# A two-layer decoder trunk on one Trainium2 core: the last two expert pairs of each layer, and the turn into the next norm

## The reference

```python
for l in range(2):
    h = h + token_mixer(rms_norm(h, ln1_g[l]), w_in[l], ...)   # u @ w_in, 4 mixers, gated merge
    h = h + hier_moe(rms_norm(h, ln2_g[l]), ..., w1[l], w3[l], w2[l])
return rms_norm(h, final_g)

# hier_moe: every token goes to the 2 best of 32 experts (within its best group of 8)
hdn = jax.nn.silu(xb @ w1[e]) * (xb @ w3[e])      # 1024 -> 256
ys  = hdn @ w2[e]                                 # 256 -> 1024
out = zeros((T + 1, D)).at[slot_tok].add(ys * slot_w[:, None])[:T]
```

## Time and profile before

| | us |
|---|---|
| median of 3 runs | 1532.07 |
| lowest, highest | 1530.59, 1535.13 |
| the profiled execution | 1531.59 |
| its span, first to last instruction | 1529.8 |

### The profile page before, as it was taken

One profiled execution on the slowest core, in us unless ns is written; L12 is line 12 of the kernel. 1 busy time (PEld: TensorE's weight loads), 2 busy tenths in 40 slices (PEclk: granted clock), 3 DMA queues, 4 the chain that ended last, 5 costly groups with the idle time before them and its releaser, 6 DMA issues.

```text
span 1529.8 us, 18813 instructions
## 1 busy us (share of the span) xinstructions
PE 1377.0 (90%) x7414; PEld 952.2 (62%) x7414; DVE 429.2 (28%) x1017; ACT 506.0 (33%) x845; POOL 495.8 (32%) x249
## 2 busy tenths in 40 slices
PE   5999999999999799787589999999999978988783
PEld 5889877788887333232278888777888863333231
DVE  3232644411214111101433335443112241111105
ACT  4522466622333111111144326665223322111111
POOL 3633433466641111110054443334656311111100
PEclk9999999999998899999899999999999979999997
DMA  7622222224363999999844222222434649999985
GB/s 241 237 84 83 70 69 76 82 84 159 122 232 140 394 417 417 415 417 413 293 172 158 84 66 93 70 69 70 149 112 154 236 198 403 416 417 417 415 340 192
DMA packets 135089, 331.80 MB, mean 217 GB/s; under 512 B 16291, under 2 KB 90067, under 8 KB 116568
## 3 DMA queue, kind: packets, MB, share of 16 engines
q1 hardware_dynamic: 124920, 310.08, 53.8%
q0 software_dynamic: 10080, 20.49, 3.5%
HBM read 312.16 MB, written 34.60 MB: 227 GB/s over the span
## 4 chain that ended last, share of the span: by engine, by line
PE 70%; SPq 16%; DMA 7%; DVE 3%; ACT 2%; issue 1%; POOL 0%; DVEq 0%; POOLq 0%; ACTq 0%
PE ps L515 17%; PE ps L516 17%; PE ps L517 17%; SPq L437 11%; PE ps L852 9%; DMA w<-in_w 5%; SPq L431 5%; PE ps L681 2%; PE ps L661 1%; PE ps L669 1%; PE ps L617 1%; DMA xg<-x_dram,toks 1%; PE ps L770 1%; DVE ut L1351 1%; PE ps L844 1%
## 5 line engine op out<-in xcount | busy, mean ns | idle before, releaser
L515 PE MATMUL ps<-uH,ringH 128*128 128x512 f32 x720 | 281.9, 392 | 0.0
L516 PE MATMUL ps<-uL,ringH 128*128 128x512 f32 x720 | 280.4, 389 | 0.0
L517 PE MATMUL ps<-uH,ringL 128*128 128x512 f32 x720 | 280.3, 389 | 0.0
L852 PE MATMUL ps<-w,xT 128*64 128x512 f32 x1024 | 243.3, 630 | 39.7 <-DMA w<-in_w 37.2
L852 PEld LDWEIGHTS ps<-w,xT 128*64 128x64 f32 x1024 | 82.0, 145 | 197.3 <-issue 193.9
L852 PE MATMUL ps<-w,hT 128*64 128x512 f32 x512 | 121.0, 616 | 52.0 <-ACT hT L1167 29.1
L1231 POOL TENSOR_TENSOR ringL<-raw,ringH 128x2048 fp32r<-128x2048 f32 (+1 forms) x31 | 138.1, 4465 | 86.5 <-ACT ringH L975 86.5
L515 PEld LDWEIGHTS ps<-uH,ringH 128*128 128x128 f32 x720 | 135.2, 188 | 29.0 <-issue 0.7
L517 PEld LDWEIGHTS ps<-uH,ringL 128*128 128x128 f32 x720 | 135.1, 188 | 28.5
L516 PEld LDWEIGHTS ps<-uL,ringH 128*128 128x128 f32 x720 | 135.2, 188 | 27.7
L1277 POOL TENSOR_TENSOR ringL<-raw,ringH 128x2048 fp32r<-128x2048 f32 x32 | 146.9, 4590 | 5.1 <-ACT ringH L1101 5.1
(11 more groups left out here) (250 smaller groups left out, 2031.9 us busy)
## 6 DMA issues: line engine op xcount, KB each, us to landing
w<-in_w SPq DMA_DIRECT2D x188, 1024.0 KB, 21.5
raw<-in_w_in SPq DMA_DIRECT2D x54, 1024.0 KB, 5.3
y_dram<-attT SPq DMA_DIRECT2D x8, 1024.0 KB, 12.1
braw<-in_w_branch SPq DMA_DIRECT2D x32, 256.0 KB, 4.4
raw<-in_w_out SPq DMA_DIRECT2D x8, 1024.0 KB, 5.2
yb<-y_dram SPq DMA_DIRECT2D x8, 1024.0 KB, 7.9
h_dram<-hs SPq DMA_DIRECT2D x2, 2048.0 KB, 11.2
hs<-h_dram SPq DMA_DIRECT2D x2, 2048.0 KB, 9.9
```

The costliest lines, as they stand in the source:

```text
L515: mm(o, h, rh, start=first, stop=False)
L516: mm(o, h, rl_, start=False, stop=False)
L517: return mm(o, l, rh, start=False, stop=last)
L852: ins = mm(o[r], lhs[:, r], rhs[x], start=first, stop=last, skip_group_check=True)
```

## The change

`NS` becomes 14, so only the pairs 0 to 13 are scattered and the read-back waits for pair 13's scatter. Pair 14's rows go the way of pair 15's: `yH`, `yL` and `tok_of` exist twice. PE multiplies the first half of the columns of pair 14 into the banks in front of its wait for the last w2 (`combine_early`), the second half together with pair 15's. SP issues `yb` as soon as pair 13's rows are stored (the last two blocks also wait for pair 14's up product), then `raw`, `g1`, and the last w2. DVE adds the first two-part row in pair 14's turn, ahead of pair 15's gate product, and makes both low halves of pair 15 ahead of the adds. In the second layer the split of unit 1 (ACT and POOL) stands ahead of the norm. The means stand ahead of the products in `first_rows`' loop. The turn of row block 3 stands ahead of the second product block of `half(0)`, in both layers.

```diff
 CAP, NW = 64, 8
-SLOTS, NS = 3, NP - 1
+SLOTS, NS = 3, NP - 2
 EPS = 1e-6
...
     yy = [sb(f"yy{x}", [P, D], f32, R_O + 4 * x * KB) for x in range(2)]
-    yH = sb("yH", [P, D], f32r, R_O + 4 * (NS % 2) * KB)
+    yH = [sb(f"yH{x}", [P, D], f32r, R_O + 4 * x * KB) for x in range(2)]
     xT = [sb(f"xT{x}", [P, D], f32, R_O + (8 + 4 * x) * KB) for x in range(2)]
...
     tok_w = sb("tok_w", [P, S], f32r, R_O + 29.25 * KB)
-    yL = sb("yL", [P, D], f32r, R_T1)
-    tok_of = sb("tok_of", [P, S], f32r, R_T1 + 8 * KB)
+    yL = [sb(f"yL{x}", [P, D], f32r, R_T1 + 4 * x * KB) for x in range(2)]
+    tok_of = [sb(f"tok_of{x}", [P, S], f32r, R_T1 + (8 + 2 * x) * KB) for x in range(2)]
     yHw = sb("yHw", [P, D], f32r, R_T1 + 12 * KB)
...
                 w13_fill(p)
-                if p < NS:
+                if p < NP - 1:
                     hold(sp, down_filled.h, down_filled.at(lay, p - SLOTS + 1))
...
-            if lay + 1 < L:
-                hold(sp, up_filled.h, up_filled.at(lay, NP - 2))
-                sp.dma_start(raw[:, 0, :].rearrange("p (k n) -> p k n", k=KD), w_in_cols(lay + 1, COL["gv"], 256)).then_inc(w_in_slot[0].h, 16)
-            hold(sp, down_filled.h, down_filled.at(lay, NP - 2))
-            sp.dma_start(g1[:], a["c_next_gain"][ds(lay, 1), :].partition_broadcast(P)).then_inc(g1_in.h, 16)
+            hold(sp, down_filled.h, down_filled.at(lay, NS))
             for x in range(2):
...
             for t in range(NT):
+                if t == 2:
+                    hold(sp, up_filled.h, up_filled.at(lay, NS + 1))
                 sp.dma_start(yb[t][:], y_dram[2 * P * t:2 * P * (t + 1), :].rearrange("(p c) n -> p c n", c=2)).then_inc(y_back[t].h, 16)
-            hold(sp, down_filled.h, down_filled.at(lay, NP - SLOTS))
+            if lay + 1 < L:
+                sp.dma_start(raw[:, 0, :].rearrange("p (k n) -> p k n", k=KD), w_in_cols(lay + 1, COL["gv"], 256)).then_inc(w_in_slot[0].h, 16)
+            sp.dma_start(g1[:], a["c_next_gain"][ds(lay, 1), :].partition_broadcast(P)).then_inc(g1_in.h, 16)
             for c in range(2):
                 for x in range(2):
-                    src = a["w2"][ds(lay, 1), ds(NS + NP * x, 1), :, c * 512:(c + 1) * 512].rearrange("o q (k p) n -> p (o q k) n", p=P)
-                    sp.dma_start(w2[NS % SLOTS][x][:, :, c * 512:(c + 1) * 512], src).then_inc(w2_last_in[c].h, 16)
+                    src = a["w2"][ds(lay, 1), ds(NP - 1 + NP * x, 1), :, c * 512:(c + 1) * 512].rearrange("o q (k p) n -> p (o q k) n", p=P)
+                    sp.dma_start(w2[(NP - 1) % SLOTS][x][:, :, c * 512:(c + 1) * 512], src).then_inc(w2_last_in[c].h, 16)
...
                         if q < 2:
-                            if 1 <= 2 * q + i < NT - 1:
-                                norm_transposes(2 * q + i + 1, rows_low)
+                            if q == 0 and i == 1:
+                                norm_transposes(2, rows_low)
                             hold(pe, rows_low.h, rows_low.at(lay, 2 * q + i + 1))
+                            if q == 0 and i == 1:
+                                norm_transposes(3, rows_low)
                         for k in range(KD):
...
+            def token_rows(y, c, t, first, last):
+                mm(bank(SUM_BANKS[c][t]), tok_of[y][:, tmc(t)], yH[y][:, c * 512:(c + 1) * 512], start=first, stop=False, skip_group_check=True)
+                return mm(bank(SUM_BANKS[c][t]), tok_of[y][:, tmc(t)], yL[y][:, c * 512:(c + 1) * 512], start=False, stop=last, skip_group_check=True)
+
+            def combine_early():
+
+                hold(pe, last_low.h, last_low.at(lay, 1))
+                hold(pe, tokens_ready.h, tokens_ready.at(lay, 1))
+                for t in range(NT):
+                    token_rows(0, 0, t, True, False)
+
             def combine_last(c):
-                hold(pe, last_low.h, last_low.at(lay, c + 1))
-                hold(pe, tokens_ready.h, tokens_ready.at(lay, 1))
+                hold(pe, last_low.h, last_low.at(lay, c + 2))
+                hold(pe, tokens_ready.h, tokens_ready.at(lay, 2))
                 for t in range(NT):
...
                         hold(pe, half_added.h, half_added.at(lay, NT))
-                    b = SUM_BANKS[c][t]
-                    mm(bank(b), tok_of[:, tmc(t)], yH[:, c * 512:(c + 1) * 512], start=True, stop=False)
-                    mm(bank(b), tok_of[:, tmc(t)], yL[:, c * 512:(c + 1) * 512], start=False, stop=True).then_inc(sum_filled.h, 1)
+                    if c:
+                        token_rows(0, c, t, True, False)
+                    token_rows(1, c, t, False, True).then_inc(sum_filled.h, 1)
...
                 pe.wait_ge(hidden_copied.h, hidden_copied.at(lay, p + 1))
-                if p < NS:
+                if p < NP - 1:
                     pe.wait_ge(w2_in[s].h, w2_in[s].at(lay, 32 * (p // SLOTS + 1)))
...
                 else:
+                    combine_early()
                     for c in range(2):
...
+            if lay:
+                split_h(1)
             for t in range(NT):
...
                 norm_h(t)
-                if t == 1:
+                if t == 1 and lay == 0:
                     split_h(1)
...
                     return
+                if p == NS:
+                    act.wait_ge(down_filled.h, down_filled.at(lay, p + 1))
+                    fn(yH[0][:], ps[:, A[0] * 512:A[0] * 512 + 1024], ACT.Copy).then_inc(last_high.h, 1)
+                    return
                 if lay + 1 < L:
...
                     act.wait_ge(last_down.h, last_down.at(lay, c + 1))
-                    fn(yH[:, c * 512:(c + 1) * 512], bank(A[c]), ACT.Copy).then_inc(last_high.h, 1)
+                    fn(yH[1][:, c * 512:(c + 1) * 512], bank(A[c]), ACT.Copy).then_inc(last_high.h, 1)
...
+            if lay:
+                split_l(1)
             for t in range(NT):
...
                     split_l(0)
-            split_l(1)
             if lay == 0:
+                split_l(1)
                 hold(pool, s_cst.h, 16 * N_CST)
...
                 norm_low(1)
-            mean_square(lay, 3)
+                mean_square(lay, 3)
             first_rows(lay, 3)
...
             def last_out_low(c):
-                dve.wait_ge(last_high.h, last_high.at(lay, c + 1))
+                dve.wait_ge(last_high.h, last_high.at(lay, c + 2))
                 cc = slice(c * 512, (c + 1) * 512)
-                v.tensor_tensor(yL[:, cc], bank(A[c]), yH[:, cc].bitcast(f32), ALU.subtract).then_inc(last_low.h, 1)
+                v.tensor_tensor(yL[1][:, cc], bank(A[c]), yH[1][:, cc].bitcast(f32), ALU.subtract).then_inc(last_low.h, 1)
...
                     return
-                slot_tokens(tok_of, slice(p, p + 1)).then_inc(tokens_ready.h, 1)
-                for t in range(NT):
+                if p == NS:
+                    dve.wait_ge(down_filled.h, down_filled.at(lay, p + 1))
+                    slot_tokens(tok_of[0], slice(p, p + 1)).then_inc(tokens_ready.h, 1)
+                    dve.wait_ge(last_high.h, last_high.at(lay, 1))
+                    v.tensor_tensor(yL[0][:], ps[:, A[0] * 512:A[0] * 512 + 1024], yH[0][:].bitcast(f32), ALU.subtract).then_inc(last_low.h, 1)
+                    sum_rows(0)
+                    return
+                slot_tokens(tok_of[1], slice(p, p + 1)).then_inc(tokens_ready.h, 1)
+                for t in range(1, NT):
                     sum_rows(t)
...
                 last_out_low(0)
-                last_row(0, 0)
-                last_row(1, 0)
                 last_out_low(1)
-                last_row(2, 0)
-                last_row(3, 0)
+                for t in range(NT):
+                    last_row(t, 0)
...
             for t in range(3):
+                mean_square(lay + 1, t + 1)
                 first_rows(lay + 1, t)
-                if t < 2:
-                    mean_square(lay + 1, t + 1)
             assert links[0] == DVE_LINKS, links
...
-        mean_square(L, 3)
         first_rows(L, 3)
```

More of the change, by code:

```diff
@@ L242, in trunk @@
     w13_in = [signal(f"w13_in{s}", 64 * len(range(s, NP, SLOTS))) for s in range(SLOTS)]
-    w2_in = [signal(f"w2_in{s}", 32 * len(range(s, NS, SLOTS))) for s in range(SLOTS)]
+    w2_in = [signal(f"w2_in{s}", 32 * len(range(s, NP - 1, SLOTS))) for s in range(SLOTS)]
     w2_last_in = [signal(f"w2_last_in{c}", 32) for c in range(2)]
@@ L293, in trunk @@
     up_filled = signal("up_filled", NP, 2); silu_ready = signal("silu_ready", NP); hidden_ready = signal("hidden_ready", NP); hidden_turned = signal("hidden_turned", NP)
-    hidden_copied = signal("hidden_copied", NP); down_filled = signal("down_filled", NS)
+    hidden_copied = signal("hidden_copied", NP); down_filled = signal("down_filled", NP - 1)
     out_first = signal("out_first", NS); out_second = signal("out_second", NS)
-    last_down = signal("last_down", 2); last_high = signal("last_high", 2); last_low = signal("last_low", 2); tokens_ready = signal("tokens_ready", 1)
```

(3 more changed lines are left out.)

## The result

The changed kernel takes 1519.66 us, median of 4 runs from 1519.63 to 1520.79; the kernel before took 1532.04 beside it (4 runs, 1530.59 to 1535.13). The ratio is 0.992, 95% interval 0.990 to 0.994: faster, inside the predicted range of 1516.0 to 1526.0 and 1.8 us under the 1521.5. Measured twice more (numbers 5 and 10), beside other runs of the kernel before, the ratio was 0.990. The profiled execution took 1519.68 us around a span of 1517.9, 11.9 us less than before.

A forecast was written before the change was run, and what follows sets the result against it. TensorE led the chain (70%), but weights from HBM set part of the span. Terms -3.7 - 3.7 - 0.2 + 0 - 2.6 + 1.8 - 2.0 = -10.4 took 1531.6 to 1521.2, plus 0.3 towards the median, 1521.5 us; range 1516.0 to 1526.0.

The forecast's parts named there:

- Part 1: End of each layer: one scatter fewer and an earlier read-back shorten the wait for the last w2 by 3.7 us.
- rival A: DMA queue before the last w2: all engines share the gap, 2.3 us more in each layer, 1516.8 us; chance 0.20.
- the late-engine sum: DMA queue before the last w2: the gap closed is the idle stretch of the engine ending last, 3.8 us per layer.
- C: Last w2 comes no sooner, as the read-back takes time from pair 15's weights and itself: 1529.0 us; chance 0.09.
- Part 2: Last w2 to the join: early products hidden in TensorE's wait, time to the first second-half add unchanged, 0 us.
- the 0.2: Layer 1's down products after w2: the clock may still be 2.4 GHz, worth 0 to 1.9 us, taken as 0.2.
- the covering wait: TensorE's wait for the last w2, taken as 9 us and expected to hide other work.
- E: Pair 15's gate product: first read-back block late, VectorE sits in front of it, slower than before; chance 0.05.
- Rival B: SP's queue: the last w2's issues are held and the queue runs dry in layer 0, 1524.0 us; chance 0.13.
- D: VectorE's adds from PSUM beside POOL's split: the split stretches an add, 1523.6 us; chance 0.05.
- Parts 3 to 5: Turn to layer 1, -2.6 us; start of layer 0, +1.8 us; last norm, -2.0 us.

The follow-up runs named there:

- number 5: The changed kernel run again with no edit: 1519.29 us, ratio 0.990 to the kernel before.
- number 10: The changed kernel run once more with no edit and profiled: 1517.6 us, ratio 0.990 to the kernel before.
- number 3: The changed kernel, but SP also waits for pair 14's low half before the read-back: 1529.75 us, ratio 0.998 to the kernel before.
- number 8: The kernel before, with the last w2 in two transfers of 4 KB pieces instead of four of 2 KB: 1534.84 us, ratio 1.001.
- number 4: The changed kernel, but SP issues the last w2 ahead of the read-back, then `yb`, `raw`, `g1`: 1521.7 us, ratio 0.991 to the kernel before.
- number 6: The changed kernel, but in layer 0 POOL splits unit 1 only after the last norm product: 1519.6 us, ratio 0.990 to the kernel before.
- number 7: The changed kernel with w2 between the read-back's blocks, VectorE's list re-ordered, next unit 0's low part on POOL, unit 1's split behind the norm: 1517.77 us.
- number 9: number 7, but POOL's split of unit 0 waits for the first PSUM add: 1515.2 us, ratio 0.988 to the kernel before.
- number 1: The changed kernel, with row block 3's turn in layer 0 back in its old place: 1516.83 us, ratio 0.988 to the kernel before.
- number 2: The kernel before, with only row block 3's turn in layer 0 moved ahead of the second product block: 1535.52 us, ratio 1.001.

## Why the prediction was right, and where it was off

**Part 1, -3.7 per layer: mechanism right, size too small.** Undone alone (number 3), it gives back 5.2 and 5.6 us in the traces. The change itself brought w2 forward by 5.24 and 6.07 us, near rival A's 6, and by the prediction's own sign of being wrong ("if w2's wait shrinks by 6 us (A)") A has it. The step that failed is "I take the late engines": the forecast counted the idle stretch of the last engine, 3.8 us. The average engine's idle time fell by 5.2 and 6.0 us (DMA share 0.58 to 0.95 and 0.55 to 0.98 of 14 us), which is what w2 gained.

The average isn't exact either: in number 3 the share of 0.50 and 0.46 gives 6.3 and 7.3 us against the changed kernel where 5.2 and 5.6 were measured, while the late-engine sum (issue of `yb` plus 2.5 us, less the start of pair 15's up product) gives 4.5 and 4.0. The truth lies between the two sums there, and at the average in the change itself. Another candidate is left for the 1.5 and 2.4 us that were missing: before, the queue went through a stretch at 241 GB/s, which number 8 prices at 1.8 and 1.9 us, while the changed kernel's queue has no 2 us under 323 until w2's first half is there. Either would fill the difference, both together would be too much, and no run separates them.

That an engine works through its ring in order, which the prediction took from the Trainium skill (DMA: Bandwidth & Descriptors, Queues, rings and completion order), is not shown by any run here and doesn't by itself lead to the late-engine sum. Rival A's own sum took thirteen engines as idle from 1482 us to the read-back, but the share of 1484 to 1486 was 0.38, so its 6 us rested on a reading that was too strong. The read-back went out at 730.85 us and not near 725.6, because pair 13's scatter itself was issued 5.1 us later (722.10 against 716.97). Two of the prediction's times are 0.1 us off their own terms (1516.9 for A, 1529.1 for C), which changes nothing.

**Part 2: right.** The first add of the second half starts 4.24 us after the first product of the join (758.33 to 762.57) against 4.23 before: 0, as taken. The clock was warm through both halves in layer 1 only: 1.94 us each, the upper bound of 1.9 in place of the 0.2. But 0.61 went to the second half of w2 and 0.85 to VectorE, which was still adding rows, so the join started only 0.33 us earlier than w2's gain explains (6.40 against 6.07). Numbers 5 and 10 had the low clock there, and the down product took 5.41 and 5.49 us, so even that is of the one execution. The early products took 3.6 us instead of 1.8 (747.01 to 750.63), at a granted clock of 0.50, and were still through before w2 came. VectorE was not late for pair 15's gate product: it waited 2.31 us for `yb`, had added the first row at 740.8, and the gate product was at 745.37. The first block came 2.4 us behind the start of pair 15's up product, as the prediction had it (2.3). Of the covering wait that it counted at some 9 us, 2.14 are left, and number 4 shows the wait of E once `yb` comes later.

**Rival B: the hold is real, its price is not.** `g1`'s issue took 7.36 us and w2's four 4.67, but from 738 to 756 every stretch of 2 us moved 334 to 426 GB/s, so the queue didn't run dry. **D: refuted.** Adds from PSUM kept 0.62 to 0.69 us each beside a split (1.28 us for the two at 762.57, the split runs from 761.25 to 763.66). The Trainium skill (SBUF — State Buffer, SBUF: two separate sides) says the same, and numbers 6, 7 and 9 agree with it from both sides: 3.38 against 1.28 and 5.45 against 1.23 us with two SBUF operands, no change with one in PSUM.

**Parts 3 to 5: right in sign and size.** Join and turn together -2.77 (forecast 0 and -2.6). Start of layer 0 +1.5 (+1.8); numbers 1, 2 and 6 show the wait and its cause. Last norm -1.7 (-2.0): the waits went from 0.76 to 0.38 and 0.44 us, not to nothing.

**What was missing.** A fall of the clock near 150 us adds 3.1 us to the profiled execution, and the pairs up to pair 15 take 0.7 us less than before. Without both rows the ledger comes to -14.3 us, and number 10's execution without the fall has a span 13.5 us under that of before, against the forecast's -10.4. That the measured time lies only 1.8 us under the prediction is partly luck: the undersized Part 1 and the unforeseen clock have opposite signs. Whether the three runs without a profile had the fall isn't known. Beside the other runs of the kernel before, the changed kernel gained 14.2 and 15.1 us (numbers 5 and 10), 4 to 5 more than the forecast's 10.4.

## What to carry to other kernels

When the last weights of a phase come late, look first at what the queue moves ahead of them. A gap there cost 5 to 6 us in each layer, about the idle time of the average DMA engine and more than that of the last one, and the cure was to issue independent transfers into it, in the order in which the slowest consumer asks. Don't place a POOL tensor operation like the split beside a VectorE one with two SBUF operands on the path (5.45 instead of 1.23 us); beside adds with one operand in PSUM it cost nothing here (3.67 us for six, with and without it). When a stall is removed, look at the granted clock behind it, for the low stretch can then fall onto the work that follows, as in number 9.

## What the runs showed of the hardware that was not expected

- The granted clock fell to 0.50 for 6.8 us between 149 and 157 us with TensorE's row showing no idle, in matmuls of the mixers; it cost 3.1 us. Of the twelve profiled executions three had it for 6.8 us and one for 3.4, and one program was seen with and without it. Executions of one kernel scatter by 1 to 10 us, and this is one visible cause. What sets it off stays open.
- The last w2 moved at 241 GB/s at its lowest in four transfers with 2 KB pieces, at 410 to 420 in two with 4 KB pieces, with the DMA engines equally busy; the difference was 1.8 and 1.9 us on 2 MB. In the changed kernel the four transfers had no such dip (323 GB/s at the lowest until the first half was there).
- POOL's split of 4.76 us stretched a VectorE add by 4.2 us, nearly the whole time for which the two overlapped (751.01 to 755.38).
